# Residual adds on VectorE, four banks in the first projection, and constant matmuls at six seams of a 256-token, three-block fp32 network

## What is computed

```
block 1:  h += rms(hgrn2(rms(h)))      w_in 1024 x 4096: q, f, i, g; gated recurrence; w_out
          h += rms(mlp(rms(h)))        mlp = relu(h @ up)^2 @ down, up 1024 x 4096
block 2:  k, v = rms(h) @ w_kv;  h += rms(diff_attention(rms(h) @ w_q, k, v) @ w_out)
          h += rms(mlp(rms(h)))
block 3:  h += rms([latent attention | gated conv](rms(h) @ w_in) @ w_out)
          h += rms((silu(rms(h) @ gate) * (rms(h) @ up)) @ down)      width 2816
          h += sigmoid(h @ w_ple_gate) * rms(p @ w_ple_proj)
rms(x) = x * rsqrt(mean(x^2) + 1e-6) * gain
```

## Time and profile before

| | us |
|---|---|
| median of 3 runs (lowest, highest) | 1101.39 (1101.08, 1104.72) |
| the profiled execution's own time | 1104.06 |
| its span | 1102.2 |
| TensorE matmuls busy | 1015.9 (92%) |
| VectorE busy | 773.4 (70%) |
| ScalarE busy | 552.9 (50%) |
| GpSimd busy | 128.7 (12%) |
| mean granted clock of TensorE | 0.971 |

### The profile page before, as it was taken

The page is one execution under the profiler, slowest core; times in us unless marked ns, Lnnn a source line. Parts: engine busy times, 40 slices in busy tenths (PEclk is TensorE's granted clock), DMA queues, the critical chain, the costliest instruction groups (busy, mean ns, idle before and its releaser), DMA issues.

```text
span 1102.2 us, 17833 instructions
## 1 busy us (share of the span) xinstructions
PE 1015.9 (92%) x6439; PEld 916.1 (83%) x6439; DVE 773.4 (70%) x1075; ACT 552.9 (50%) x826; POOL 128.7 (12%) x122
## 2 busy tenths in 40 slices
PE   5899988999999889887899999987998799999987
PEld 5799987788888779775788888987997688888876
DVE  4587675987644596774698764468866988776466
ACT  4553255565444453453555544444456555555444
POOL 5023201200000220000130000203001310000020
PEclk9899999899999999998999999999999899999999
DMA  8343334376666426800447655534533456665641
GB/s 244 110 132 116 115 118 150 96 210 190 191 191 191 153 93 213 248 0 1 134 135 214 187 189 185 188 100 110 168 116 91 119 160 204 189 190 172 200 144 58
DMA packets 163754, 165.82 MB, mean 150 GB/s; under 512 B 6736, under 2 KB 161504, under 8 KB 163696
## 3 DMA queue, kind: packets, MB, share of 16 engines
q1 hardware_dynamic: 162496, 163.47, 48.9%
q0 software_dynamic: 1056, 1.16, 0.5%
q10 hardware_dynamic: 144, 0.39, 0.1%
HBM read 163.92 MB, written 1.08 MB: 150 GB/s over the span
## 4 chain that ended last, share of the span: by engine, by line
PE 77%; DVE 10%; issue 9%; ACT 2%; POOL 1%; DMA 0%; DVEq 0%; ACTq 0%; POOLq 0%
PE ps L567 30%; PE ps L566 15%; PE ps L563 4%; PE ps L780 3%; PE ps L546 2%; PE ps L544 2%; PE ps L545 2%; PE ps L550 2%; PE ps L552 2%; PE ps L551 2%; PE ps L564 2%; DVE w_lo L1692 2%; PE ps L869 1%; PE ps L868 1%; DVE mo L1792 1%
## 5 line engine op out<-in xcount | busy, mean ns | idle before, releaser
L1692 DVE TENSOR_TENSOR w_lo<-w_raw,w_hi 128x1024 fp32r<-128x1024 f32 (+3 forms) x318 | 387.5, 1224 | 174.0 <-ACT w_hi L1211 170.3
L1211 ACT ACTIVATE w_hi<-w_raw 128x1024 fp32r<-128x1024 f32 x302 | 317.6, 1054 | 217.7 <-PE ps L567 106.2
L567 PE MATMUL ps<-xs,w_hi 128*128 128x512 f32 x938 | 336.0, 400 | 0.0
L566 PE MATMUL ps<-xs,w_lo 128*128 128x256 f32 x938 | 265.3, 283 | 0.5 <-DVE xs L1823 0.5
L567 PEld LDWEIGHTS ps<-xs,w_hi 128*128 128x128 f32 x938 | 178.9, 191 | 39.5
L566 PEld LDWEIGHTS ps<-xs,w_lo 128*128 128x128 f32 x938 | 180.1, 192 | 5.0 <-DVE xs L1823 1.3
L567 PE MATMUL ps<-us,w_hi 128*128 128x512 f32 x498 | 175.3, 394 | 0.0
L566 PE MATMUL ps<-us,w_lo 128*128 128x256 f32 x498 | 140.8, 283 | 0.0
L2523 POOL TENSOR_TENSOR sq<-sq 128x512 f32<-128x512 f32 x30 | 48.3, 1611 | 685.3 <-ACT sq L1268 605.0
L550 PE MATMUL ps<-xs,w_hi 128*128 128x256 f32 x320 | 96.2, 301 | 16.3 <-DVE w_lo L1692 6.9
L567 PEld LDWEIGHTS ps<-us,w_hi 128*128 128x128 f32 x498 | 93.5, 188 | 21.2
(11 more groups left out here) (361 smaller groups left out, 1701.5 us busy)
## 6 DMA issues: line engine op xcount, KB each, us to landing
w_raw<-in_mlp_w_up SPq DMA_DIRECT2D x64, 512.0 KB, 4.2
w_raw<-in_mlp_w_down SPq DMA_DIRECT2D x64, 512.0 KB, 3.5
w_raw<-in_a_w_in SPq DMA_DIRECT2D x32, 512.0 KB, 3.8
w_raw<-in_w_gate SPq DMA_DIRECT2D x22, 512.0 KB, 3.8
w_raw<-in_w_up SPq DMA_DIRECT2D x22, 512.0 KB, 4.7
w_raw<-in_w_down SPq DMA_DIRECT2D x20, 512.0 KB, 4.0
w_raw<-in_w_kv SPq DMA_DIRECT2D x16, 512.0 KB, 3.4
w_raw<-in_w_in SPq DMA_DIRECT2D x16, 512.0 KB, 3.8
```

Source lines behind the costliest of these rows:

```text
L566: mm(ps[:, bank, 0:S], lo[:, kk, w], x[:, kt, 0:S], start=False, stop=False)
L567: o = mm(ps[:, bank, :], hi[:, kk, w], x[:, kt, :], start=False, stop=last)
L1211: o = fn(dst, raw, ACT.Copy)
L1692: return v.tensor_tensor(d, x, y, ALU.subtract)
```

## The change

1. **Adds.** `add` of GpSimd is gone. VectorE adds tiles 4 and 5, then 6 and 7, as two 512-column adds in `post`. One semaphore `h_tile` replaces three.
2. **Sums.** GpSimd adds no more squares for `kv_b`, `mix_pre`, `ple` and `f_pre`; TensorE sums those with eight matmuls. For `m0_pre` and `m1_pre` GpSimd still adds, but only once `up` is done, and TensorE's two matmuls stand behind the first pair of `down`. Their norm is cut to two VectorE instructions (`mlp_norm`); ScalarE's two are gone. The counters of norms are split into `MEAN` and `ROOT`.
3. **First projection.** Units go through four banks; unit n waits for n - 4 (three exceptions at the end). The second quantum of unit 2 is split before the first norm. Angles and sines move into `down0`. The outputs of heads 4 to 7, the gates and the first high and low parts stand one quantum or so earlier.
4. **Constant matmuls.** `keep_streaming(9)` follows `sums` at each seam: nine float32 matmuls of the identity by 256 columns of the table, into bank 6, which nothing reads there.

```diff
+def unit_bank_of(n):
+    return {13: 1, 14: 0, 15: 3}.get(n, n % 4)
+def freed_by(n):
+    return {13: 10, 14: 13, 15: 12}.get(n, n - 3)
...
-PRE_ADDED = [x for x, pairs in NORM_LIST if pairs == 4 and x not in ("x", "sub")]
+RAW_NORMS = ("m0_pre", "m1_pre")
+PRE_ADDED = POSTS + list(RAW_NORMS)
...
+            def keep_streaming(n):
+                for _ in range(n):
+                    mm(ps[:, B6, 0:S], ident, table[:, T_IDENT:T_IDENT + S], start=True, stop=True)
...
-                bank = 3 if n == UNIT0["g3"] else n % 2
+                bank = unit_bank_of(n)
                 if part == 0:
-                    pe.wait_ge(unit_taken, n - 1)
+                    wait(pe, unit_taken, freed_by(n))
...
-                if q == 28:
+                if q == 27:
                     head_outputs(1)
                 if q == 29:
                     turn_heads(0)
-            turn_heads(1)
+                if q == 30:
+                    turn_heads(1)
...
             sums("a_post")
-            stream("up0", xs, pairs=16, waits=xs_wait("m0"), after=lambda: sums("m0_pre"), two=True)
+            keep_streaming(9)
+            stream("up0", xs, pairs=16, waits=xs_wait("m0"), two=True)
...
+            stream("down0", us, per=4, waits=us_wait(0), last_kt=FF // P - 1, first_pair=lambda: sums("m0_pre"))
             sums("m0_post")
+            keep_streaming(9)
...
             act.wait_ge(eps_ready, 1)
+            hi_q(5)
             root("x")
-            hi_q(5)
...
             def mlp_norm(name):
-                norm(name)
+                dve.wait_ge(sq_used, SQ0[name] + 4)
+                v.tensor_scalar(ms[:, :], ps[:, NS, 0:S], 1.0 / D, EPS, ALU.mult, ALU.add).then_inc(ms_ready, 1)
+                dve.wait_ge(ms_ready, MEAN[name] + 1)
                 v.scalar_tensor_tensor(fold[:, :], ms[:, :], EPS * D / P, ms[:, :], ALU.mult, ALU.mult).then_inc(fold_ready, 1)
...
+                for t in (4, 6):
+                    weigh(mo, mo, wcol, t)
+                    link(weigh(mo, mo, wcol, t + 1))
+                    v.tensor_tensor(h[:, t:t + 2, :], h[:, t:t + 2, :], mo[:, t:t + 2, :], ALU.add).then_inc(h_tile, 2)
+                    if t == 4:
+                        low_tile(3)
+                        lo(following + 1, part=1)
                     low_tile(t)
+                    low_tile(t + 1)
...
             lo_q(4)
+            lo_q(5)
             first_norm()
             small_work()
-            lo_q(5)
+            lo_q(6)
             small_work2()
-            lo_q(6)
...
-            product_to_mo("down0", per=4)
+            product_to_mo("down0", per=4, between={1: angles, 5: lambda: mlp_norm("m0_pre"), 9: turns})
...
-            def add(r):
-                for j in (2, 3):
-                    pool.wait_ge(scaled, 2 * r + j - 1)
-                    pr = slice(2 * j, 2 * j + 2)
-                    g.tensor_tensor(h[:, pr, :], h[:, pr, :], mo[:, pr, :], ALU.add).then_inc(h_ready, 1)
```

More of the change, by code:

```diff
@@ L918, in _ @@
             sums("b_post")
-            stream("up1", xs, pairs=16, waits=xs_wait("m1"), after=lambda: sums("m1_pre"), two=True)
-            stream("down1", us, per=4, waits=us_wait(16), last_kt=FF // P - 1)
+            keep_streaming(9)
+            stream("up1", xs, pairs=16, waits=xs_wait("m1"), two=True)
+            stream("down1", us, per=4, waits=us_wait(16), last_kt=FF // P - 1, first_pair=lambda: sums("m1_pre"))
             sums("m1_post")
+            keep_streaming(9)
             pe.wait_ge(p_in, 16)
@@ L1219, in copy_second, with steps @@
                 o.then_inc(pair_copied, 1)
-            def steps(name, per=1, pairs=4, body_pairs=2, peel=0, post=None, copies=True, scale=1.0, root_of=None):
+            def steps(name, per=1, pairs=4, body_pairs=2, peel=0, post=None, copies=True, scale=1.0):
                 u0, p0 = UNIT0[name], PAIR0[name]
@@ L1236, in body @@
                             post(i * body_pairs + b, b)
-                    if root_of is not None and isinstance(i, int) and i == 0:
-                        root(root_of)
-                peel = max(peel, int(root_of is not None))
                 times(act, pairs // body_pairs, body, peel)
@@ L1441, in deep_to_mo @@
                     square(post_name, j, mo[:, 2 * j:2 * j + 2, :], pair_summed, p0 + j + 1)
+                    if j == 0 and turns is not None:
+                        turns()
             def up_post(first):
@@ L1451, in _, with turns @@
             residual("a_post", "m0_pre", 0, V_M0_PRE)
-            steps("up0", pairs=16, post=up_post(0), root_of="m0_pre")
-            deep_to_mo("down0", 4, "m0_post")
+            steps("up0", pairs=16, post=up_post(0), peel=1)
+            def turns():
+                act.wait_ge(ang_ready, 1)
+                fn(sin[:, :], ang[:, 2, :], ACT.Sin)
+                fn(cos[:, :], ang[:, 3, :], ACT.Sin).then_inc(rope_ready, 1)
+                root_tables()
+            deep_to_mo("down0", 4, "m0_post", turns)
             residual("m0_post", "kv_b", 1, V_KV)
@@ L1501, in _ @@
             residual("b_post", "m1_pre", 2, V_M1_PRE)
-            steps("up1", pairs=16, post=up_post(16), root_of="m1_pre")
+            steps("up1", pairs=16, post=up_post(16), peel=1)
             deep_to_mo("down1", 4, "m1_post")
@@ L2555, in _ @@
                 pool.wait_ge(aq_zero, m + 1)
-            add(1)
-            add_squares("kv_b")
-            pool.wait_ge(sq_added, ADD0["kv_b"] + 3)
             pool.wait_ge(hankel_in, 16)
@@ L2563, in _ @@
             add_squares("b_post")
-            add(2)
-            add_squares("m1_pre")
             p_src = a["p_2"][0, 0]
@@ L2568, in _ @@
             pool.dma_start(prow[:, :, :], p_src.rearrange("(m p) n -> p m n", p=P)).then_inc(p_in, 16)
+            pool.wait_ge(w_used, 2 * UNIT0["down1"])
+            add_squares("m1_pre")
             add_squares("m1_post")
-            add(3)
-            add_squares("mix_pre")
             pool.wait_ge(p_turned, 1)
@@ L2579, in _ @@
             pool.wait_ge(rope_spread, 1)
-            add_squares("ple")
             add_squares("mix_post")
-            add(4)
-            add_squares("f_pre")
             add_squares("f_post")
-            add(5)
 _INS = ["x", "a_norm_pre", "a_norm_post", "a_w_in", "a_lb", "a_gate_norm", "a_w_out", "kv_norm", "w_kv",
```

130 lines of the change are left out of this document (59 added, 71 removed).

## The result

| | before | changed |
|---|---|---|
| median, us | 1102.7 (4 runs, 1101.08 to 1104.72) | 1089.56 (4 runs, 1087.67 to 1093.24) |
| ratio, 95% interval | | 0.9883 (0.9861 to 0.9905) |
| profiled execution, us | 1104.06 | 1087.67 |
| its span | 1102.2 | 1085.5 |
| gaps of TensorE over 0.25 us, summed | 75.9 | 44.3 |

The change gains 1.17%, 12.9 us of 1102.7. The two profiled executions differ by more, 16.7 us of span, because that of the changed kernel was the fastest of its four. I use that pair for where the time went and the ratios for how much. The three other executions of the changed kernel had mean granted clocks of 0.988 to 0.990; where theirs fell, no trace shows.

The account below looks back on a forecast made before the run. TensorE was taken as the bound, its time being work plus gaps. Seams 9.6 + first projection 7.5 + its end 0 - sums 7.3 = 9.8 us gained, from the median 1101.4 to 1091.6 us; the forecast's own range was 1088.5 to 1095.

Parts of the forecast that it names:

- Nine constant matmuls fit and hold the clock: Six seams: nine take 4.1 us, leave 0.7 us of gap, delay no restart and keep the granted clock at 1.00.
- slower: Rival, chance 0.05: constant matmuls at 1.2 GHz run past the gap, restart 3.3 us late; about 1105.
- Tiles in 12.3 us, 1.6 gained each: Eight tiles behind the restart take 12.3 us for 13.9: 1.6 us gained at five seams, 1.4 at the last.
- Each edit needs the other: Seams: with the old clock, the same faster-fed tiles would end at 13.7 us instead of 12.3.
- The first projection, 7.5: Opening: four banks remove a 4.5 us wait, and 6.1 us at clock 0.50 become 3.05; 7.5 us gained.
- ScalarE did not hold it: Rival at the opening, chance 0.13: late handovers or another table load lose half of the 7.5 us; 1095.5.
- cover in `down0`: Moved angles and sines hide under TensorE's units in down0; without that cover they would cost 6.5 us.
- The end of the projection: First projection's last unit is taken at about the old time: 0, bounds 1 us lost and 2.5 gained.
- more is hidden: Rival, chance 0.15: first projection's end keeps its clock (2), mix_pre and kv_b lie beside other waits (3); 1087.
- The sums, 7.3 lost: TensorE's sums: f_pre 2.7, mix_pre 2.7, kv_b 1.4 and m0_pre with m1_pre 1.5 lost, ple 1.0 gained.
- the other 1.5: m0_pre and m1_pre: their two matmuls no longer cover a bank wait and come in down, 0.75 us lost each.
- clock falls nevertheless: Rival, chance 0.10: small gaps still drop the clock, seams give 0.2 us each instead of 1.6; about 1100.

## Why the prediction was right, and where its steps were not

The time (1089.56 for 1091.6), the side and the range held. The gain was 12.9 us where the sum had 9.8; the time is nearer than the gain because the kernel before has its median at 1102.7 over the four runs, not at 1101.4. The parts by steps:

- **Nine constant matmuls fit and hold the clock: right.** 4.05 us, gaps of 0.87 to 0.97 at five seams and 0.39 at the fourth, clock 1.00 at all six, and at all six in the profiles of the six other kernels that have nine or twelve constants in the changed seams. The rival "slower" needed constants at half clock, and none of these traces has them.
- **Tiles in 12.3 us, 1.6 gained each: mis-sized a little.** It was 11.96 (858.54 to 870.50), and the stretches with the sum 1.95 to 2.0 shorter. At the last seam it was 1.4 as forecast (13.0 to 11.6).
- **"Each edit needs the other": right, and more than I wrote.** Without the constants 9.4 of 12.9 us go (I had 8.4). With the constants alone the kernel is slower, which no step of mine had: the half clock was hidden behind the slow tiles, and the constants turned it into gaps with a fall behind two of them.
- **The first projection, 7.5: right (7.8 at the first step).** ScalarE did not hold it: TensorE has no wait between 40 and 53. But I gave the gain to the banks and named the angles as cover in `down0` only. The runs show that they are halves: banks alone nothing, banks with angles 7.6, all but the banks 8.7 short. The end of the projection, put at 0 with bounds to 2.5, gave 2.0: that is the first condition of the rival "more is hidden", and it came true. The measured time lies between the forecast and that rival's 1087.
- **The sums, 7.3 lost: the wrong account.** In place, six more matmuls cost 2.2 us, not 2.7 (`f_pre`), and the stretch from `kv_b`'s sum to the first scores grew by 3.0 (1.4 in my sum), half of it the new fall at 397.6: with four constants and with the adds back on GpSimd the same wait of 2.6 us is there without a fall behind it, and the stretch grew by 1.5 and 1.4 (66.94 and 66.86 for 65.45). That looks like the loss I wrote down. But putting the four sums back, for which I had 5.8 us, changes nothing: GpSimd's squares slow VectorE by 2.0 us at each of the three seams that have them again. For `m0_pre` and `m1_pre`, the other 1.5, no run was made. I credited the seams' 1.6 to GpSimd's adds and the clock and booked the sums as pure cost; the squares' move is part of what makes the tiles fast. The earlier trace rows had it in sight, the 2.32 us of `w_lo`; I did not read on to the low parts that ran beside the squares, 4.38 us for three.
- **Not in my sum:** from the first scores to `b_post` the changed kernel takes 75.9 us instead of 79.0, with the same work. The clock fell there three times before and once in the changed trace. It makes up for the 3.0 that the stretch ahead of it lost, so that the stage gains just the seam's 2.0. The other traces say that it comes with the execution and not with the change: the part takes 75.3 to 75.9 us in four traces with one fall in it, 77.4 in one with two and 78.4 to 79.9 in nine with three or a longer first one, among them 79.7 with four constants and 79.5 with two banks, whose orders there are those of the changed kernel. Part of the 16.7 us between the two profiles is thus luck.

The rival "clock falls nevertheless" (1100) did not come at nine constants, but it did at four: single seams fell and others not, as it said. The Trainium skill (TensorE: Matmul & The Clock Gate, Part 1) has the clock judged free of the kernel's start. These traces agree: with four constants, a gap of 3.12 us was followed by a fall at two seams and by none at a third, in one execution.

## What to carry to other kernels

In this kernel a low clock cost time only where TensorE had work waiting (0 us at three seams, 1.5 at two others). Filling a gap with unread matmuls paid when the stream behind it was well fed (9.4 us), and was lost, or worse, when the gap only moved in between late tiles (5.4 us slower). So first speed up what feeds the stream, then fill the gap, and measure both together and each alone. Before paying on TensorE for work taken off GpSimd, look at what VectorE does beside it: the price and the gain can be equal and both unseen in a total. And compare places in two traces from a mark that both share: one execution here ran 2.4 us ahead from its start, and its first step looked as early as the changed kernel's.

## What was not expected of the hardware

In these traces VectorE is not slowed in part beside GpSimd: its instruction takes longer by nearly what was left of GpSimd's. An add of 0.69 us took 1.69, with 1.1 left of GpSimd's; two scalings of 0.87 took 1.91, with 1.2 left; a low part of a weight 2.31 for 1.22, with 1.2 left. The Trainium skill (SBUF — State Buffer, section SBUF: two separate sides) describes a pair of ports that the two engines share, which one instruction holds to its end while the other engine's is blocked; a VectorE instruction with two inputs in SBUF counts among them against a GpSimd one that reads SBUF. The durations here agree. In the changed kernel six gaps of 4.3 to 4.9 us, filled with float32 matmuls of a constant by a constant, kept the clock at 1.00 as real work does. And the same stage took the same time in different kernels within 0.03 us, so that a stage table between two single profiles can find effects of 0.1 us as long as the clock does not fall in it.
